# Dilated layer: more q/k tiles turned by DMA, another score order, earlier high and low halves

## The reference

```python
DIL_PATTERNS = ((128, 1), (512, 4), (2048, 16))      # window, dilation; 16 heads of 64

def dilated_mixer(a, cos, sin, w_in, w_o):
    proj = (a @ w_in).reshape(B, S, N_DIL, 3, H, DH)
    for gi, (window, dil) in enumerate(DIL_PATTERNS):
        q = partial_rope(proj[:, :, gi, 0], cos, sin)
        k = partial_rope(proj[:, :, gi, 1], cos, sin)
        v = proj[:, :, gi, 2]
        o, lse = banded_attention(to_residue(q, dil), to_residue(k, dil), to_residue(v, dil), window // dil)
        ...
    alpha = jax.nn.softmax(jnp.stack(lses, axis=-1), axis=-1)
    o = jnp.einsum('bshn,bshnd->bshd', alpha, jnp.stack(outs, axis=3))
    return o.reshape(B, S, H * DH) @ w_o
```

## Time and profile before

| | us |
|---|---|
| median of three runs (lowest, highest) | 805.84 (805.14, 805.84) |
| the profiled execution | 805.32 |
| its span, first to last instruction | 803.6 |
| TensorE busy | 791.9 |
| VectorE busy | 536.7 |
| ScalarE busy | 452.2 |
| GpSimd busy | 160.8 |

### The profile page before, as it was taken

One profiled execution on the slowest core, in us unless ns is written; L12 is line 12 of the kernel. 1 busy time (PEld: TensorE's weight loads), 2 busy tenths in 40 slices (PEclk: granted clock), 3 DMA queues, 4 the chain that ended last, 5 costly groups with the idle time before them and its releaser, 6 DMA issues.

```text
span 803.6 us, 11763 instructions
## 1 busy us (share of the span) xinstructions
PE 791.9 (99%) x4337; PEld 636.5 (79%) x4337; DVE 536.7 (67%) x1085; ACT 452.2 (56%) x843; POOL 160.8 (20%) x248
## 2 busy tenths in 40 slices
PE   9999999999999999999999999999999999999996
PEld 7877676788888888788887788887778888888885
DVE  6956969796565556697567665776668775656544
ACT  7836887764444345474565665565658554445331
POOL 1000005812211222004304202403400112211110
PEclk9999999999999999999999999999999999999999
DMA  9955211168987587669647637555834688677801
GB/s 317 357 185 202 86 54 53 49 189 242 233 228 200 176 225 236 182 186 251 214 156 170 197 116 219 152 196 133 230 122 163 205 223 221 179 204 235 226 24 53
DMA packets 145401, 146.42 MB, mean 182 GB/s; under 512 B 42768, under 2 KB 128832, under 8 KB 145216
## 3 DMA queue, kind: packets, MB, share of 16 engines
q1 hardware_dynamic: 107760, 132.53, 53.3%
q10 hardware_dynamic: 36576, 8.94, 7.0%
q0 software_dynamic: 1008, 4.19, 1.4%
HBM read 134.64 MB, written 2.10 MB: 170 GB/s over the span
## 4 chain that ended last, share of the span: by engine, by line
PE 94%; DVE 3%; ACT 2%; issue 1%; POOL 0%; ACTq 0%; POOLq 0%
PE ps L1900 85%; PE ps L1909 5%; PE ps L2177 2%; PE ps L2150 2%; PE ps L2188 1%; DVE probs_dil L1564 1%; PE ps L1962 0%; ACT stage_dil L1158 0%; ACT junk L811 0%; DVE w_lo L1336 0%; ACT xd_hi L799 0%; ACT w_hi L790 0%; ACT probs_b L962 0%; DVE h L1660 0%; DVE h L1666 0%
## 5 line engine op out<-in xcount | busy, mean ns | idle before, releaser
L1336 DVE TENSOR_TENSOR w_lo<-w_raw,w_hi 128x1024 fp32r<-128x1024 f32 x240 | 301.2, 1281 | 60.6 <-ACT w_hi L790 58.8
L790 ACT ACTIVATE w_hi<-w_raw 128x1024 fp32r<-128x1024 f32 x240 | 245.7, 1058 | 27.5 <-issue 22.1
L1900 PE MATMUL ps<-w_hi,xt_hi 128*128 128x512 f32 x472 | 188.5, 401 | 0.3 <-ACT w_hi L790 0.3
L1900 PE MATMUL ps<-w_hi,xt_lo 128*128 128x512 f32 x472 | 183.5, 390 | 0.0
L1900 PE MATMUL ps<-w_lo,xt_hi 128*128 128x512 f32 x472 | 183.0, 390 | 0.0
L1900 PE MATMUL ps<-w_hi,xd_hi 128*128 128x512 f32 x288 | 116.8, 406 | 0.2 <-DVE w_lo L1336 0.2
L1900 PE MATMUL ps<-w_hi,xd_lo 128*128 128x512 f32 x288 | 113.0, 393 | 0.0
L1900 PE MATMUL ps<-w_lo,xd_hi 128*128 128x512 f32 x288 | 112.7, 391 | 0.0
L1900 PEld LDWEIGHTS ps<-w_hi,xt_hi 128*128 128x128 f32 x472 | 88.5, 188 | 25.1 <-issue 8.6
L1900 PEld LDWEIGHTS ps<-w_hi,xt_lo 128*128 128x128 f32 x472 | 88.6, 188 | 18.8
L1900 PEld LDWEIGHTS ps<-w_lo,xt_hi 128*128 128x128 f32 x472 | 88.7, 188 | 16.6 <-DVE w_lo L1336 0.3
(11 more groups left out here) (274 smaller groups left out, 1001.4 us busy)
## 6 DMA issues: line engine op xcount, KB each, us to landing
w_raw<-in_ffn_w_gu SPq DMA_DIRECT2D x88, 512.0 KB, 5.9
w_raw<-in_dil_w_in SPq DMA_DIRECT2D x72, 512.0 KB, 4.7
w_raw<-in_ffn_w_down SPq DMA_DIRECT2D x44, 512.0 KB, 5.3
w_raw<-in_nsa_w_in SPq DMA_DIRECT2D x20, 512.0 KB, 7.7
w_raw<-in_nsa_w_o SPq DMA_DIRECT2D x8, 512.0 KB, 4.7
w_raw<-in_dil_w_o SPq DMA_DIRECT2D x8, 512.0 KB, 4.8
w_k<-in_nsa_cmp_wk SPq DMA_DIRECT2D x2, 1024.0 KB, 9.4
w_raw<-in_nsa_cmp_wv SPq DMA_DIRECT2D x2, 1024.0 KB, 11.7
```

Source lines behind the costliest of these rows:

```text
L790: act.activation(w_hi[:, n.slot, c:c + 1024], w_raw[:, n.slot, c:c + 1024], ACT.Copy)\
L1336: dve.tensor_tensor(w_lo[:, n.slot, c:c + 1024], w_raw[:, n.slot, c:c + 1024], w_hi[:, n.slot, c:c + 1024].bitcast(F32), ALU.subtract)\
L1900: ins = pe.matmul(o, s, m, start=start, stop=stop, **kw)
```

## The change

21 of the 24 QK tiles are turned by transfers: all six of group 0, and in groups 1 to 3 all but the last (dilation four, m = 1), which stays with TensorE. DIL_BARS is 21 and PE_TURNS 3 (tiles 17, 27 and 35). GpSimd's list runs over five or six tiles of a group with the same rule: split the following tile, then merge this one. `merge_qk` gets the shift by one key column that dilation four needs, with two small copies more for m = 0. The first pair of a group waits separately for each pattern's merges (`merges_until`), and a pair's scores are made in the order of dilations one, two, four; the count of `scores` moves to dilation four's last product. The high and low halves of dilation one are made two steps after the group's second tile of that pattern (FIRST_DONE: steps 7, 17, 27, 35, which in groups 1 to 3 is the step of the group's last tile), on ScalarE before the second half of the weight piece, on VectorE at the end of the step. TensorE gets one more wait ahead of the output projection. Cut to its core:

```diff
-DIL_BARS = 2 * MT * DIL_G
+DIL_BARS = 6 + 5 * (DIL_G - 1)
 ...
-BARS = [x for x in TILES if x.kind == QK and x.pat < 2]
-PE_TURNS = [x for x in TILES if x.kind == QK and x.pat == 2]
+FIRST_DONE = [max(x.e for x in TILES if x.g == g and x.kind == QK and x.pat == 0) + 2 for g in range(DIL_G)]
+PE_TURNS = [x for x in TILES if x.kind == QK and x.g and x.pat == 2 and x.m]
+BARS = [x for x in TILES if x.kind == QK and x not in PE_TURNS]
 ...
+def merges_until(g, pats):
+
+    return max(bar_at(x) for x in BARS if x.g == g and x.pat in pats) + 1
 ...
 # GpSimd
-                        first, second, third, fourth = [x for x in BARS if x.g == g]
-                        split_qk(first)
-                        split_qk(second)
-                        merge_qk(first)
-                        split_qk(third)
-                        merge_qk(second)
-                        split_qk(fourth)
-                        merge_qk(third)
-                        merge_qk(fourth)
+                        of_group = [x for x in BARS if x.g == g]
+                        split_qk(of_group[0])
+                        for x, following in zip(of_group, of_group[1:]):
+                            split_qk(following)
+                            merge_qk(x)
+                        merge_qk(of_group[-1])
 ...
 # ScalarE
             def first_hi_out(g):
-                act.wait_ge(ht_merged, len(XBAR) + 4 * (g + 1))
+                act.wait_ge(ht_merged, merges_until(g, (0,)))
 ...
                 split(n + k, (0,))
-                if TILES[e].g > TILES[e - 1].g:
-                    first_hi_out(TILES[e - 1].g)
                 dil_attend(2 * e)
 ...
                 dil_planes(TILES[e - 1])
                 dil_turn_out(TILES[e - 1])
+                if e in FIRST_DONE:
+                    first_hi_out(FIRST_DONE.index(e))
                 if e > 4:
                     split(n + k, (1,))
 ...
             dil_evac(TILES[-1])
             split(n + 3, (0,))
-            first_hi_out(DIL_G - 1)
             dil_turn_out(TILES[-1])
 ...
 # VectorE
-                if TILES[e].g > TILES[e - 1].g:
-                    first_lo_out(TILES[e - 1].g)
                 if e > 4:
                     split(n + k, (1,))
                 dil_attend(2 * e + 1, True)
+                if e in FIRST_DONE:
+                    first_lo_out(FIRST_DONE.index(e))
 ...
             dil_rope(TILES[-1])
             split(n + 3, (0,))
-            first_lo_out(DIL_G - 1)
             dil_mask(3, 0)
 ...
 # TensorE, dil_scores: the block over pat in (1, 2) moves behind dilation one's products
+                for pat in (1, 2):
+                    if t == 0:
+                        pe.wait_ge(ht_merged, merges_until(g, (pat,)))
+                        if g and pat == 2:
+                            pe.wait_ge(turn_out[1], g)
 ...
+                            if pat == 2 and cls == 1:
+                                ins.then_inc(scores[1], 1)
 ...
+            pe.wait_ge(proj_out[1], LAST_E - 1)
             o_dil(0, 0, (0, 1, 2))
             dil_turn(TILES[-1])
             o_dil(0, 0, (3, 4, 5))
```

More of the change, by code:

```diff
@@ L130, in xbar_of @@
     tiles = [x for x in XBAR if x[1] == m]
-    return (len(tiles) + DIL_BARS // 2) * layer + tiles.index((j, m)) + 1
+    return (len(tiles) + (DIL_BARS + 1 - m) // 2) * layer + tiles.index((j, m)) + 1
 TILES = dil_tiles()
 LAST_E = len(TILES)
-BARS = [x for x in TILES if x.kind == QK and x.pat < 2]
-PE_TURNS = [x for x in TILES if x.kind == QK and x.pat == 2]
+FIRST_DONE = [max(x.e for x in TILES if x.g == g and x.kind == QK and x.pat == 0) + 2 for g in range(DIL_G)]
+PE_TURNS = [x for x in TILES if x.kind == QK and x.g and x.pat == 2 and x.m]
+BARS = [x for x in TILES if x.kind == QK and x not in PE_TURNS]
 def bar_at(x):
     return len(XBAR) + BARS.index(x)
+def merges_until(g, pats):
+    return max(bar_at(x) for x in BARS if x.g == g and x.pat in pats) + 1
 def pair_start(g, t):
@@ L735, in merge_qk @@
                     k = at + 2 * 2 * S + plane + 2 * 64 * x.m
-                    ins = pool.tensor_copy(u16_at(whole, k, [[2 * S, 2], [2 * P, 2], [2, 64]]),
-                                           view(planes_qt, src + 512 * plane + 256, [[P, 2], [1, 2], [2, 64]]))
+                    k_src = src + 512 * plane + 256
+                    first = int(x.pat == 2 and x.m == 0)
+                    if first:
+                        pool.tensor_copy(u16_at(whole, k + 2 * (P - 1), [[2 * S, 2], [2 * P, 2], [2, 1]]),
+                                         view(planes_qt, k_src, [[P, 2], [1, 2], [2, 1]]))
+                    shift = int(x.pat == 2) - first
+                    ins = pool.tensor_copy(u16_at(whole, k - 2 * shift, [[2 * S, 2], [2 * P, 2], [2, 64 - first]]),
+                                           view(planes_qt, k_src + 2 * first, [[P, 2], [1, 2], [2, 64 - first]]))
                 ins.then_inc(ht_merged, 1)
@@ L1198, in dil_turn_out @@
                 at, src = at + 2 * S, src + 2 * P
[L1199 to L1206, removed]
+                ins = act.activation(view(qk_t, at + x.m * 64 - 1, [[S, 2], [P, 2], [1, 64]]),
+                                     view(ps, src, [[P, 2], [1, 2], [2, 64]]), ACT.Copy)
                 ins.then_inc(turn_out[1], 1)
             def first_hi_out(g):
-                act.wait_ge(ht_merged, len(XBAR) + 4 * (g + 1))
+                act.wait_ge(ht_merged, merges_until(g, (0,)))
                 for hi, _, src in first_parts(g):
@@ L1250, in _ @@
             dil_planes(TILES[0])
-            dil_turn_out(TILES[1])
+            dil_planes(TILES[1])
             dil_evac(TILES[2])
@@ L2509, in dil_scores @@
                     pe.wait_ge(masked[1], ws[0])
-                if t == 0:
-                    pe.wait_ge(ht_merged, len(XBAR) + 4 * (g + 1))
-                    pe.wait_ge(turn_out[1], 2 * (g + 1))
                 js = (2 * hp, 2 * hp + 1)
[L2514 to L2520, removed]
                 if t == 0:
@@ L2527, in dil_scores @@
                 for j, w in zip(js, ws):
-                    mm(bank(score_bank(w), 0, S), first_q(g, j, m)[1], first_k(g, j)[0], False, True)\
-                        .then_inc(scores[1], 1)
+                    mm(bank(score_bank(w), 0, S), first_q(g, j, m)[1], first_k(g, j)[0], False, True)
+                for pat in (1, 2):
[3 more added lines that the diff above has]
+                            pe.wait_ge(turn_out[1], g)
+                    for cls in range(2):
+                        for j, w in zip(js, ws):
+                            c = cls if pat == 1 else 1 - cls
+                            ins = mm(ps[64 * cls:64 * cls + 64, score_bank(w), 256 + c:DIL_N:2],
+                                     head(g, pat, 0, j, m * P + 64 * cls, 64), head(g, pat, 1, j, m * P + c, 64, 2),
+                                     True, True)
+                            if pat == 2 and cls == 1:
+                                ins.then_inc(scores[1], 1)
             def dil_turn_probs(w):
```

## The result

The changed kernel takes 817.11 us, the median of five runs (815.09 to 817.69), beside 805.84 of the kernel before (805.14 to 805.95): a ratio of 1.0138, with a 95% interval from 1.0125 to 1.0152 (ratios and intervals here are taken over all runs of both kernels, and so are not quite the quotients of the medians).

What follows compares the result with a forecast made beforehand. TensorE bounds the kernel, busy 791.9 us of a 803.6 us span. 805.3 - 2.2 (turns) + 8.1 (waits) + 1.2 (collision) = 812.4, say 812.5 us; stated range 807 to 817, with chance 0.75.

Steps and rivals of the forecast that it cites:

- the sum's own range: Whole kernel: the summed terms at their low and high ends, 807.5 to 815.5 us.
- the clock's rival: TensorE's clock falls to half after each of three waits, 5.4 us on top, 818 us; chance 0.08.
- Turns removed, -2.2: TensorE: five tiles lose their four turns, 0.45 us a tile, 2.2 us gained.
- The chain: ScalarE and VectorE work queued behind GpSimd's merge delays each group's last rotation; 10.80 us long in group 1, 10.20 in group 2.
- the three waits: TensorE waits for the late rotations of tiles 17, 27 and 35: 2.8, 1.8 and 3.5 us, together 8.1.
- The collision, +1.2: GpSimd's dilation-four merge can fall on VectorE's low halves and last rotation: 0.4 us for each of three places.
- Their order does: GpSimd's added splits and merges hold nobody up by themselves; taking the following tile's split ahead of a merge does.
- Group 0, taken as 0: No turns left on TensorE there, and four value tiles come before the next group: no loss.
- Score order, 0: 16 pairs make the same products in another order: taken as 0, bounded by 1.6 us either way.
- the dilation-four merge, hidden: Group 3's first pair: the new wait hides this merge; without that wait it could cost 2.6 us.

Runs made afterwards that it cites:

- e3: The changed kernel, but VectorE makes the low halves after the rotation of the group's last tile instead of before it; 810.34 us, ratio 1.0059.
- e9: The changed kernel, but ScalarE makes the weight piece's high half ahead of the high halves in the group's last tile; 808.03 us, ratio 1.0028.
- e6: The changed kernel, but in groups 1 to 3 GpSimd merges dilation one's second tile before splitting the first dilation-four tile; 818.82 us, ratio 1.0159.
- e2: The changed kernel with 26, 13 and 33 idle turns filling TensorE's three waits for the late rotation; 814.03 us, ratio 1.0103.
- e4: The kernel before with only the score order changed to dilations one, two, four; 806.07 us, ratio 1.0003.
- e5: The changed kernel with ScalarE's high halves last in the group's last tile and VectorE's low halves behind the late rotation; 805.69 us, ratio 1.0008.
- e11: The changed kernel unaltered, profiled once more; that execution took 817.66 us.
- e7: The changed kernel unaltered, run again with a profile; 816.36 us, ratio 1.0127.
- e10: The changed kernel with 33 idle turns on TensorE ahead of the third late wait only; 815.48 us, ratio 1.0115.

## Why the prediction was right, and what it missed

**The whole.** The slowdown came, by the mechanism that was forecast. The size is another matter: the median lies 4.6 us above 812.5 and 1.6 above 815.5, the upper end of the sum's own range. That the stated range reaches as far as the result is owed to the half of the clock's rival that was taken into it, and not to the sum.

**Turns removed, -2.2.** The shifts give -2.19 for five tiles. That size came from the earlier trace rows and held.

**The chain.** From the rotation of tile 16 to the end of the rotation of tile 17 it took 11.29 us in group 1 (450.69 to 461.98), where 10.80 and a part of the 0.4 were forecast. Split and merge take 3.63 (451.64 to 455.27) against 3.61, high halves and the piece's high half 2.19 against 2.23. Group 2 took 10.12 against 10.20, group 3 11.28 against 10.80. The order of the three waits, third longest and second shortest, came as forecast, and e3 and e9 take out single links and shorten the waits, by 1.2 to 1.8 us where 1.8 was expected and by 1.4 to 2.0 where 2.2 was. The waits of 3.3, 1.9 and 4.1 exceed the forecast 2.8, 1.8 and 3.5 by what the next term counts, so their sum, 9.3 us, is the sum of the two terms 8.1 and 1.2.

**The collision, +1.2.** In groups 1 and 3 the merge of the dilation-four tile fell on the late rotation, which took 1.44 instead of 0.88; in group 2 it was over in time. Twice 0.56 is 1.1: the size was right, but it lies in two places and not in three. The 0.4 for each place was a middle value between 0 and 0.9 that no row singled out, so that the total fits is luck.

**One sentence was right as a description and wrong as a cause.** "Their order does" puts the loss on GpSimd taking the split ahead of the merge. e6 turned that order round and lost more. The delay is the sum of merge and split behind one rotation, in either order.

**Group 0, taken as 0.** It lost 0.45 us. There is no late turn there, but the same wait of ScalarE for a merge delays the evacuation of a value tile; ScalarE and then TensorE:

```profile
391.07 0.73 ACT L1216 ACTIVATE q_hi<-qk_t 128x256 fp32r<-128x256 f32 x2 [1.74 <-POOL qk_t L748]
...
393.52 0.83 ACT L1175 ACTIVATE v<-ps,rs_v 128x256 f32<-128x256 f32 x2
```

```profile
394.40 0.19 PEld L1901 LDWEIGHTS ps<-w_hi,xd_hi 128*128 128x128 f32 x1 [0.56 <-ACT v L1175]
```

I had looked at turns only, and not at everything queued behind the moved step.

**The clock, a rival at 0.08, came true in part.** It was priced at 1.8 us a wait, from 3.6 us at half clock that no row of the prediction shows; a stretch of half clock cost 1.7. What failed was its treatment as all or nothing. In the three traces of the changed kernel one or two of three waits were followed by it, so 1.7 to 3.4 belong to the likeliest case. With them and group 0 the sum is 805.8 - 2.2 + 9.3 + 0.45 + 1.7 to 3.4 = 815.1 to 816.8, where the changed kernel's medians are 816.4 and 817.1. The Trainium skill (TensorE: Matmul & The Clock Gate, "HAM oscillation") tells of clock lost to gaps in which TensorE idles; e2 agrees, where the granted clock is 1.00 with the gaps filled.

**Score order, 0,** and **the dilation-four merge, hidden.** e4 bears out the first. The second held in the changed kernel only because the waits cover it, as the prediction said: without them group 3's first pair waits 0.8 us for that merge by the profile (e5), less than the 2.6 that it could have cost.

## What to carry to other kernels

Where a step is moved ahead in an engine's program and brings a wait with it, list everything that is queued behind that wait on its engine and on the engines that feed on it, and follow it to the first instruction that the bounding engine needs; put the waiting step last in its slot, or put the work that is ready ahead of it. A wait of a few us on TensorE can cost more than its length: add the price of a stretch at half clock to the likeliest case and not only to a rival. A version that keeps only the places where the cover is long enough (here 20 transfers, halves late) can win a little, 1.6 us here, where the whole change loses 11.3.

## What the runs showed of the hardware

Whether half clock followed a wait was not told by the length of the idle time alone. In the changed kernel's profiled run TensorE was idle 3.15 us in the first wait and kept 2.4 GHz, while in e3 2.2 us of idle time in the third place was followed by half clock. The place has a part: the third wait was followed by it in all six traces in which it left TensorE idle for 2 us or more (the changed kernel's three, e3, e6 and e9), the first in e11 (3.39 us idle) and e6 (3.78) but not in the profiled run, e7 and e10 (3.15 to 3.17), the second in e6 alone (2.86). What decides it is open. Each such stretch cost about 1.7 us, but for e6's third: (1 - 0.54) x 6 = 2.8.

VectorE and GpSimd stretch each other in both directions. The low half of a weight piece took 2.05 us beside a split and 1.23 without, and GpSimd's copy beside it 1.47 instead of 0.48.

A transfer of the changed kernel takes longer to land than before, 3.0, 5.6 and 9.2 us (least, median, most) against the last row:

```profile
DMA to landing us min/median/max: 3.0/5.6/9.2
```
